# Narrow part of an expert first, wide part second, in a one-core diffusion backbone with a top-2-of-8 expert layer

## What is computed

```python
def moe_swiglu(h, router_w, w_in, w_out):            # h: (1, 256, 1024)
    logits = jnp.einsum('btd,de->bte', h, router_w).astype(jnp.float32)
    top_vals, top_idx = lax.top_k(logits, TOP_K)     # 2 of 8
    gates = jax.nn.softmax(top_vals, axis=-1)
    combine = jnp.sum(jax.nn.one_hot(top_idx, N_EXPERTS, dtype=jnp.float32) * gates[..., None], axis=-2)
    out = jnp.zeros_like(h)
    for e in range(N_EXPERTS):
        out = out + combine[..., e:e + 1].astype(h.dtype) * swiglu(h, w_in[e], w_out[e])
    return out
```

## Time and profile before

| what | value |
|---|---|
| median of 3 runs | 1671.93 us (1671.19 to 1673.8) |
| the profiled execution's own time | 1671.87 us |
| its span, first to last instruction | 1670.0 us |
| TensorE busy in the span | 1583.0 us (95%) |
| VectorE / ScalarE / GpSimd busy | 519.8 / 391.1 / 34.5 us |
| bytes moved by DMA | 474.42 MB, mean 284 GB/s |

### The profile page before, as it was taken

The page is one execution under the profiler, slowest core; times in us unless marked ns, Lnnn a source line. Parts: engine busy times, 40 slices in busy tenths (PEclk is TensorE's granted clock), DMA queues, the critical chain, the costliest instruction groups (busy, mean ns, idle before and its releaser), DMA issues.

```text
span 1670.0 us, 28575 instructions
## 1 busy us (share of the span) xinstructions
PE 1583.0 (95%) x12596; PEld 953.8 (57%) x12596; DVE 519.8 (31%) x791; ACT 391.1 (23%) x655; POOL 34.5 (2%) x70
## 2 busy tenths in 40 slices
PE   5999989999999989998899999999999998999986
PEld 2855678878788877866536333463435533345232
DVE  3427467665533276357500010100101001010012
ACT  3327342221232243248400111000100001100011
POOL 1000100010000000000000000000000000000000
PEclk9999999999999999999899999999999999999998
DMA  9661816676523323213699999999999999999995
GB/s 368 210 226 36 258 51 202 199 256 231 217 85 120 117 82 126 101 51 138 253 318 390 417 418 421 417 419 418 418 421 418 419 418 418 420 418 419 418 418 213
DMA packets 106754, 474.42 MB, mean 284 GB/s; under 512 B 11176, under 2 KB 35144, under 8 KB 70784
## 3 DMA queue, kind: packets, MB, share of 16 engines
q1 hardware_dynamic: 103552, 467.64, 72.0%
q0 software_dynamic: 3072, 4.88, 1.1%
HBM read 471.36 MB, written 1.13 MB: 283 GB/s over the span
## 4 chain that ended last, share of the span: by engine, by line
PE 64%; SPq 19%; DMA 9%; DVE 5%; issue 2%; ACT 1%; DVEq 0%; ACTq 0%
PE ps L1140 62%; SPq L601 13%; SPq L598 6%; DMA w_moe<-in_expert_out_w_dram 2%; DMA work<-in_expert_out_w_dram 2%; DMA w_raw<-in_expert_out_w_dram 2%; DMA work<-in_expert_in_w_dram 1%; DMA w_raw<-in_ada_w_dram 1%; DMA w_moe<-in_expert_in_w_dram 1%; PE ps L1323 1%; DVE work L1835 1%; PE ps L1654 1%; DVE row_max L2103 1%; DVE w_lo L1766 0%; SPq L596 0%
## 5 line engine op out<-in xcount | busy, mean ns | idle before, releaser
L1140 PE MATMUL ps<-w_hi,h_t 128*128 128x512 f32 (+1 forms) x960 | 294.6, 388 | 11.5 <-DVE h_t L1824 5.4
L1140 PE MATMUL ps<-h_t,w_hi 128*128 128x512 f32 (+1 forms) x768 | 222.5, 374 | 6.2 <-DVE h_t L1824 6.2
L1140 PEld LDWEIGHTS ps<-w_hi,h_t 128*128 128x128 f32 x960 | 180.8, 191 | 49.0 <-issue 4.1
L1766 DVE TENSOR_TENSOR w_lo<-w_raw,w_hi 128x2048 fp32r<-128x2048 f32 x57 | 130.6, 2292 | 228.3 <-ACT w_hi L738 227.9
L1140 PE MATMUL ps<-w_lo,h_t 128*128 128x512 f32 (+1 forms) x480 | 185.4, 386 | 0.0
L2290 DVE TENSOR_TENSOR residual<-residual,ps 128x1152 f32<-128x1152 f32 (+3 forms) x15 | 19.4, 1292 | 529.1 <-PE ps L1140 529.1
L738 ACT ACTIVATE w_hi<-w_raw 128x2048 fp32r<-128x2048 f32 x57 | 108.9, 1913 | 301.7 <-PE ps L1140 301.4
L1140 PE MATMUL ps<-w_moe,h_te 128*32 128x512 f32 (+2 forms) x1830 | 170.6, 520 | 5.3 <-DMA w_moe<-in_expert_in_w_dram 4.4
L1140 PE MATMUL ps<-w_raw,h_te 128*32 128x512 f32 (+2 forms) x1694 | 159.5, 519 | 7.0 <-DMA w_raw<-in_expert_in_w_dram 6.1
L1140 PEld LDWEIGHTS ps<-h_t,w_hi 128*128 128x128 f32 x768 | 141.3, 191 | 33.8 <-issue 9.2
L1140 PE MATMUL ps<-work 128*32 128x512 f32 (+6 forms) x1104 | 141.9, 498 | 11.4 <-DMA work<-in_expert_out_w_dram 5.0
(11 more groups left out here) (274 smaller groups left out, 1210.2 us busy)
## 6 DMA issues: line engine op xcount, KB each, us to landing
w_raw<-in_ada_w_dram SPq DMA_DIRECT2D x48, 1024.0 KB, 5.3
w_raw<-in_expert_in_w_dram SPq DMA_DIRECT2D x43, 1024.0 KB, 24.7
w_moe<-in_expert_in_w_dram SPq DMA_DIRECT2D x42, 1024.0 KB, 26.1
w_raw<-in_expert_out_w_dram SPq DMA_DIRECT2D x40, 1024.0 KB, 23.7
work<-in_expert_in_w_dram SPq DMA_DIRECT2D x37, 1024.0 KB, 23.4
w_moe<-in_expert_in_w_dram SPq DMA_DIRECT2D x45, 768.0 KB, 22.0
work<-in_expert_out_w_dram SPq DMA_DIRECT2D x33, 1024.0 KB, 23.8
w_moe<-in_expert_out_w_dram SPq DMA_DIRECT2D x33, 1024.0 KB, 23.5
```

What stands on the lines that cost most here:

```text
L1140: return pe.matmul(out_, l, r, start=first, stop=last, skip_group_check=True)
L1766: dve.tensor_tensor(WLO[:, b % SPL, :], WRAW[:, slot_w[b], :], WHI[:, b % SPL, :].bitcast(F32), ALU.subtract).then_inc(lo_done, 1)
```

## The change

The names A and B keep their places in the order, and their widths are exchanged. A, which is worked first, now has 1536 columns and 6 output blocks; B, worked second, has 2048 columns and 8 output blocks. So in all four lists the passes GA and UA are made of 0.75 MiB blocks and GB and UB of 1 MiB blocks. The counts in `AFTER`, the splits of the output blocks (3 + 3 for A, 4 + 4 for B), the tile numbers and the cases in `in_block`, `hidden` and the transposes follow. Which columns of the weights belong to which part follows too: A takes columns 0 to 1535 of G and of U.

```diff
-WIDTH = {"A": 2048, "B": 1536}
-OUTS = {"A": 8, "B": 6}
+WIDTH = {"A": 1536, "B": 2048}
+OUTS = {"A": 6, "B": 8}
...
-LAST = in_pass("GB") + out_blocks("A", 0, 4) + in_pass("UB") + out_blocks("A", 4, 8)
-CYCLE = LAST + in_pass("GA", 1) + out_blocks("B", 0, 3) + in_pass("UA", 1) + out_blocks("B", 3, 6)
-LAST = LAST + out_blocks("B", 0, 6)
-AFTER = {"GB": 8, "UB": 20, "GA": 32, "UA": 43}
+LAST = in_pass("GB") + out_blocks("A", 0, 3) + in_pass("UB") + out_blocks("A", 3, 6)
+CYCLE = LAST + in_pass("GA", 1) + out_blocks("B", 0, 4) + in_pass("UA", 1) + out_blocks("B", 4, 8)
+LAST = LAST + out_blocks("B", 0, 8)
+AFTER = {"GB": 8, "UB": 19, "GA": 30, "UA": 42}
...
     def tiles(cap, half):
-        return {(CAP, "A"): 12, (CAP, "B"): 9, (SMALL, "A"): 8, (SMALL, "B"): 6}[cap, half]
+        return {(CAP, "A"): 9, (CAP, "B"): 12, (SMALL, "A"): 6, (SMALL, "B"): 8}[cap, half]
...
-                r0 = 256 * b + (2048 if what == "B" else 0)
+                r0 = 256 * b + (1536 if what == "B" else 0)
                 rows = expert_out_w[0, e, r0:r0 + 256, :]
-                if cap == CAP and what == "B" and b in (3, 4):
+                if cap == CAP and what == "A" and b in (3, 4):
...
-                n = 512 if half == "A" or b < 2 else P
+                n = 512 if half == "B" or b < 2 else P
                 for tg in range(3):
                     piece(tg, b, 0, n, tg, 512 * b)
-                if half == "A":
+                if half == "B":
                     ins = piece(3, b, 0, 512, b, 1536)
...
-                    if (what, b) == (("A", 5 if early else 7) if last else ("GA", 1)):
+                    if (what, b) == (("A", 4 if early else 5) if last else ("GA", 1)):
                         transposes(e, "B")
```

More of the change, by code:

```diff
@@ L539, in tile_at @@
     def tile_at(cap, half):
-        return 8 if cap == SMALL and half == "B" else 0
+        return 6 if cap == SMALL and half == "B" else 0
     def tiles(cap, half):
-        return {(CAP, "A"): 12, (CAP, "B"): 9, (SMALL, "A"): 8, (SMALL, "B"): 6}[cap, half]
+        return {(CAP, "A"): 9, (CAP, "B"): 12, (SMALL, "A"): 6, (SMALL, "B"): 8}[cap, half]
     QKV_BANK = {n: (0, 1, 4, 5) if n in (0, 3, 5) else (4, 5) if n == 1 else (2, 3, 6, 7) for n in range(6)}
@@ L599, in fetch @@
             else:
-                c0 = (0 if what[0] == "G" else ED) + (0 if what[1] == "A" else 2048)
+                c0 = (0 if what[0] == "G" else ED) + (0 if what[1] == "A" else 1536)
                 sp.dma_start(w, expert_in_w[0, e, b * P:(b + 1) * P, c0:c0 + WIDTH[what[1]]]).then_inc(done, 16)
@@ L1061, in silu @@
                     for b in range(3):
-                        act.activation(SIL[:, 512 * b:512 * b + 512], ps[:, b, :],
+                        n = 512 if b < 2 else P
+                        act.activation(SIL[:, 512 * b:512 * b + n], ps[:, b, 0:n],
                                        ACT.Silu).then_inc(silu_half if b < 2 else silu_done, 1)
@@ L1605, in out_block @@
                 first = half == "A" and m == 0 and j == 0
-                last = half == "B" and m == 5 and j == 1
+                last = half == "B" and m == 7 and j == 1
                 for tg in range(3):
@@ L1652, in transposes @@
                 for x in range(tiles(cap, half)):
-                    src = pairs[:, x // 2, x % 2, :] if cap == SMALL or half == "A" or x < 6 else SIL[:, P * x:P * x + P]
+                    src = pairs[:, x // 2, x % 2, :] if cap == SMALL or half == "B" or x < 6 else SIL[:, P * x:P * x + P]
                     ins = pe.transpose(ps[:, 5 + x // 4, P * (x % 4):P * (x % 4) + P], src, ID[:])
@@ L2285, in product @@
                     for b in range(3):
-                        part = slice(512 * b, 512 * b + 512)
+                        part = slice(512 * b, 512 * b + (512 if b < 2 else P))
                         dve.tensor_tensor(SIL[:, part], SIL[:, part], PSF[:, part],
```

## The result

The changed kernel takes 1676.91 us (median of 19 runs, 1675.99 to 1680.34) against 1672.99 us for the kernel before (19 runs, 1670.96 to 1676.32). Over all runs the ratio is 1.0026, with a 95% interval of 1.0018 to 1.0033: slower by about 4.3 us (3.0 to 5.5 us; the medians alone are 3.9 us apart). 4.2 us were forecast. The profiled execution has a span of 1674.6 us against 1670.0 us. Both programs have 28575 instructions and move 474.42 MB.

A forecast was written before the change was run, and what follows sets the result against it. DMA at its ceiling was taken to set the end, after a slot-limited stretch in the first expert. 924.4 + 288.25 x 2.515 = 1649.3 against 1645.1 us gives +4.2: 1671.9 + 4.2 = 1676.1 us, range 1671.9 to 1680.5 us.

The forecast's parts named there:

- Where it becomes the bound for good: End of A5, first expert, at 924.4 us: block 55 issues, 288.25 MiB left, 1649.3 against 1645.1 us, +4.2 us.
- Last landing: Arrival of the last weight block, forecast near 1658 us, with 11 to 13 us of closing work behind it.
- The first passes: GA and UA of the first expert free slots faster; DMA at its ceiling from 831 us, some 8 us behind after UA.
- The slot limit comes back: From GB the 8 us backlog melts, gone near 892 us; DMA waits for slots until A5 ends, losing the earlier gain.
- Less is fetched ahead: Before the first expert the 18 slots hold 14 MiB instead of 17.5 MiB; by itself +8.8 us.
- The account of the kernel before: 300 MiB from block 40's issue at 890.56 us, DMA never resting: 1645.1 us; last landing 8.7 us later.
- Small edits and the tail: Transposes in the first expert's GA' pause TensorE 0.4 us more, taken as 0; end of kernel 0, between -2 and +2 us.
- Rival 1: DMA stays at its ceiling throughout from 831 us: -4.8 us, 1667.1 us; chance 8%.
- Rival 2: Loss given back elsewhere, by a tail shorter by some us or a lag counting fully: about +1 us, 1673 us; chance 17%.
- Rival 3: Full price: the 3.0 MiB lag at 930 us is no backlog, both kernels lag alike: +8.2 us, 1680.1 us; chance 14%.
- rival 4: Small transfers in single file: the 11 0.75 MiB blocks before A5 fall back 1.4 us each: +15 us more, 1691 us; chance 1%.
- The second way in the working: Compares full rings at 930.0 and 924.4 us: +8.2 us, less 4.3 to 4.8 us for lag, leaves +3.4 to +3.9 us.

The follow-up runs named there:

- the cut kernels: First expert's products cut to 11/16 of their columns, in the kernel before (1661.42 us, ratio 0.9926) and in the changed kernel (1668.03 us, ratio 0.9968).
- four late blocks: Kernel before with the last four of 18 blocks fetched ahead held until block 0 is used: 1672.84 us against 1673.54 us, ratio 0.9997.
- the other seven alone: Changed kernel with only the first expert put back to wide part first: 1679.18 us, ratio 1.0034 to the kernel before.
- the first experiment: Kernel before with only the first expert worked narrow part first: 1669.68 us against 1673.54 us, ratio 0.9977.
- the order loaded early: SP's loads of the experts' order moved ahead of block 18: kernel before 1672.09 us (ratio 0.9997); with the first expert narrow first 1668.56 us (0.9977).

## Why the prediction was right, step by step

- *What bounds.* Right. DMA at its ceiling sets the end from the first expert's end on. The ceiling is 417.3 GB/s now (294.23 MB in 705 us) against 416.9.
- *Where it becomes the bound for good.* Right to the step: end of A5 forecast for 924.4 us, and GA'0 starts at 923.63 us; the issue that it allows, block 55, is at 924.02 us. The difference is the earlier start of the experts (827.87 against 828.48 us), which varied from execution to execution (827.49 to 832.27 us among these nine profiles). 49.23 MiB were in by 930 us, inside the window of 48.5 to 50 that was to confirm the price. DMA came to its ceiling later than I said, though: I named 928 us, and it moved 308 GB/s in 925 to 930 us and 387 in 930 to 935 us.
- *Last landing.* Forecast near 1658 us, measured 1658.41 us. From the sum's 1649.3 us that is 9.1 us, against 8.7 us in the kernel before. That forecast and measurement agree to 0.1 us is chance, since the interval is 2.5 us wide. The mechanism is confirmed by the other kernels, not by this digit.
- *The first passes.* Right: DMA moved 421 GB/s in 840 to 870 us. Their use took 32.4 us, with a wait of 0.8 us in it (16 x 1.96 us alone are 31.4 us, not the 32.1 us of the text).
- *The slot limit comes back.* Right that it does, and that this decides the sign; the cut kernels show both halves. Its shape was wrong. I put the trough at 892 to 925 us with 300 to 350 GB/s. The mean of this stretch is 323 GB/s, but it is 394 in 892 to 910 us and 239 in 910 to 925 us. The backlog did end about when I said: blocks issued in 890 to 895 us land after 5.9 us. But four of the blocks released then, B0 to B3, are of 1 MiB, and 1 MiB each 2.60 us is 403 GB/s (an estimate from the prices), close to the ceiling; the 0.75 MiB blocks come after them. Then comes the gather, a pause of 3.8 us that stands in the earlier trace rows and that I left out of this part. The sum was not touched, since it rests on the end of A5 and on the ring's content, and not on how DMA gets there.
- *Less is fetched ahead: "by itself +8.8 us".* Wrong as a cause. With the later slot limit in place it costs nothing that can be measured (four late blocks), and 17.5 MiB put back bring nothing (the other seven alone). It has a price, some 6.6 us between the cut kernels, where no slot limit follows. The term was not in my sum, but the text reads as if it were the loss.
- *What I missed.* The change is two changes of opposite sign, and the prediction did not split them. The first expert narrow first gives 3.8 us. Narrow GA' and UA' in the ring while it is worked then take some 8 us (from the first experiment to the changed kernel, where the sums give 1649.3 - 1641.2 = 8.1 us), and 5.6 us where the first expert is wide first. The difference of 3.8 and 8 us is the result.
- *The account of the kernel before.* It starts at 890.56 us, after SP's delay, as if the delay counted in full. It does not: without it block 36 gives 1644.3 us, and the measured effect of taking it away is -0.5 us (-2.3 to +1.3 us). So 1645.1 us stands to within 0.8 us.
- *Small edits and the tail.* The transposes' pause shows in the issues: block 57 at 926.60 us, block 58 at 929.52 us, where their distance is otherwise 1.29 us. By the sum block 58 gives 929.52 + 286 x 2.515 = 1648.8 us, no later than block 55 with 924.02 + 288.25 x 2.515 = 1649.0 us, so by the sum 0 was right for it. No run prices the pause alone. The tail stayed: 7.0 and 7.2 us beyond the account. The closing work is 16.2 us and not 11 to 13 us; I misread the chain there, and it is equal on both sides. The chain of waits first leaves TensorE at 1140.4 us, earlier than 1144.4 us, as forecast.
- *The rivals.* Rival 1 is a real mechanism with its condition absent. Rival 2 needed a shorter tail, and the tail did not shorten. Rival 3 would have needed 8.2 us, rival 4 15 us more. The fit of the Trainium skill from which rival 4 came ("DMA: Bandwidth & Descriptors", Anatomy of one DMA) is given there for DMAs that GpSimd issues, and these are issued by SP; the 313 GB/s of the earlier trace rows decide. The second way in the working (+3.4 to +3.9 us) was a little low, within the interval of 3.0 to 5.5 us.

The best kernel here is the first experiment, with or without the order loaded early: 1669.68 us, 3.8 us faster than before and, by the two ratios, about 8 us faster than the changed one.

## What to carry to other kernels

A prefetch ring with a fixed number of slots holds blocks, not bytes: a small block in a slot is room thrown away in the very stretch where the consumer is the slower side. For each block whose issue waits for a slot, take the moment of the issue, count the bytes that are then still to come, and multiply by the transfer rate. The block with the latest result sets the end, but for the tail. Here that is one of the last that waited. What was fetched before that moment, early or late, drops out. If the consumer is slow in one stretch only, put its cheap blocks there and let the ring fill with large ones, and leave everything else as it is.

## What the runs showed of the hardware that was not expected

The first 5 us after a rest of DMA are low even where slots come free fast enough. In the changed kernel, with 1 MiB released every 1.96 us, 830 to 835 us reads 275 GB/s. In steps of 1 us this is 8, 180, 377, 442 and 369 GB/s after the issue at 830.07 us: most of the loss is the first 2 us, before the bytes flow, and no slow climb. The next window, 835 to 840 us, still reads 354 GB/s at a DMA share of 0.98, and from 840 us on it is 421. No run shows what holds it at 354.

The transfers in flight can hide a gap of 3 us in SP's issues: the block issued before it takes 7.9 us to land, and taking the gap away changed the time by less than can be measured (-2.3 to +1.3 us).
